# Hybrid decoder block: x in four half loads, row 0 ahead of the last transposes, and gated scores joined to the keys' transposes

## The chip, the cores and the metric

The kernel runs on one core of a Trainium2 chip. The metric is the device time of one execution in microseconds (us), lower is better. The kernel before was timed in three runs.

## What is computed

One decoder block over 256 tokens of width 1024, all in float32. Cut to what matters here:

```
h    = rms_norm(x, norm1_gain)              # x is 256 x 1024
proj = h @ w_in                             # 1024 x 3088, the first product
gq, gk, gv, gr, g_low, mq, mk, mv = split(proj)
log_a = log_sigmoid(g_low @ w_gate_up + b_gate) / 16
o_gla = gla_chunked(gq, gk, gv, log_a)      # gated linear attention, 4 heads: scores q_dec . k_inv, masked, times v
o_moba = attention(rotary(mq), rotary(mk), mv)   # 4 heads, causal over 256 tokens
x = x + concat(norm(o_gla) * silu(gr), norm(o_moba)) @ w_out
x = x + (silu(h2 @ w_gate) * (h2 @ w_up)) @ w_down    # h2 = rms_norm(x)
return rms_norm(x, final_norm_gain)
```

## The kernel before, in words

Every large product is done in three TensorE passes over fp32r parts: the left side is kept as a high and a low part (aT_hi, aT_lo), and so is each weight (w_hi, w_lo). A weight lands in a buffer `raw`, ScalarE casts it to w_hi, VectorE subtracts to get w_lo. Each product is therefore a triple hi*hi, hi*lo, lo*hi, of 512 columns each. Weights come in units of 2048 columns for each partition; raw has 3 slots and w_hi, w_lo have 6. A unit of w_in is 24 such matmuls for the two token tiles t = 0 and t = 1.

The order on each engine is written out by hand, and each engine waits on semaphores. There is no scheduler. The places that this study speaks of:

- The start. SyncE's queue issues x as two loads of 128 rows (`x_loaded`, L338), then the first eight rows of w_in one by one (`load_first`, L334): row 0 at once, rows 1 to 7 only when token tile 0 of x has landed. ("Row n" is one load of 128 x 512 weights.)
- TensorE first runs `warm_up` (L527), matmuls on constants whose result nobody reads, while x is on its way. Then it transposes x by 128 x 128 blocks into the aux banks (`x_transposed`, L535): block k of tile t goes to bank k // 2. Between the two tiles stand two small transposes, of norm1_gain (L543) and of the rotary frequencies (L546).
- ScalarE squares tile 0 (L885), then multiplies the transposed blocks by the gain into aT_hi (`take_xT`, L902), both token tiles of block k in one instruction, when the bank of both tiles is complete (`xT_in_psum`). VectorE makes w_hi and w_lo of row 0 (L1172, L1174) and aT_lo (L1157).
- `first_row(k)` (L564, L567, L570) multiplies block k of x by row k: two matmuls hi*hi, two hi*lo, two lo*hi. Behind row 0 stand `angle_inputs` (L553, L555), two small transposes.
- After row 7 come `gate_low` (L589), `other_gains` (L579), and then the units 2 to 11 of w_in (`in_unit`, L510 to L512). Between the matmuls of a unit's tile 0 and tile 1, or behind the unit, stand the attention steps, by the tables `midway` and `after`: `moba_k_transposed` (L613, eight 128 x 128 transposes of the rotated keys) midway in unit 7, and `gla_scores` (L650) behind it, `moba_scores` (L661, L665) midway in unit 8.
- gla_scores multiplies heads of 64 rows, so its weights are 64 partitions high. It waits for `glaT_ready`, which ScalarE signals after its copies L958. VectorE masks the result into a_gla (L1293, semaphore `a_ready`), and moba_scores waits for that, since it writes the same banks, and for `mT_q_ready` (ScalarE L975).

Of the kernel before, what the change touches and what calls it, by code (L numbers as in the profile page):

```python
# [22 lines left out]
P = 128  # L23
SEQ, D = 256, 1024
T = SEQ // P
# [67 lines left out]
def build_block(nc, x, positions, norm1_gain, w_in, w_gate_up, b_gate, gla_out_gain, moba_out_gain,  # L93
# [6 lines left out]
    with ExitStack() as ctx:  # L100
        def sb(name, shape, dt=f32):
            return ctx.enter_context(nc.sbuf_tensor(name, [P, *shape], dt))

        def sem(name):
            return ctx.enter_context(nc.semaphore(name))
# [8 lines left out]
        x_sb = sb("x_sb", [T, D])  # L114
# [93 lines left out]
        ang, turns, turns_lo, sin_arg = (reuse_e[:, n * T * HALF:(n + 1) * T * HALF] for n in range(4))  # L208


        x_loaded = [sem(f"x_loaded_{t}") for t in range(T)]
        rows_loaded = sem("rows_loaded")
        norm1_loaded = sem("norm1_loaded")
        low_loaded = sem("low_loaded")
# [117 lines left out]
        def _(sp):  # L332
            def load_first(n):
                sp.dma_start(raw[:, n // 4, (n % 4) * 512:(n % 4 + 1) * 512],  # L334
                             w_in[0, n * P:(n + 1) * P, BLOCKS[0]:BLOCKS[0] + 512]).then_inc(first_loaded[n], 16)

            for t in range(T):
                sp.dma_start(x_sb[:, t, :], x[0, t * P:(t + 1) * P, :]).then_inc(x_loaded[t], 16)  # L338
            load_first(0)
            sp.wait_ge(x_loaded[0], 16)  # L340
            for n in range(1, KC):
                load_first(n)

# [162 lines left out]
        def _(pe):  # L506
# [17 lines left out]
            def warm_up(n):  # L524

                for _ in range(n):
                    nc.tensor.matmul(acc[:, 2, 0:SEQ], warm[:, 0:P], warm, start=True, stop=True)  # L527

            warm_up(16)
            pe.wait_ge(ident_built, 1)  # L530

            def x_transposed(t, banks):
                for bank in banks:
                    for k in (2 * bank, 2 * bank + 1):
                        last = nc.tensor.transpose(aux[:, bank, (k % 2) * SEQ + t * P:(k % 2) * SEQ + (t + 1) * P],  # L535
                                                   x_sb[:, t, k * P:(k + 1) * P], ident[:, :])
                    if t == T - 1:
                        last.then_inc(xT_in_psum, 1)

            pe.wait_ge(x_loaded[0], 16)  # L540
            x_transposed(0, range(4))
            pe.wait_ge(norm1_loaded, 16)
            nc.tensor.transpose(acc[:, 3, NORM1_ROW:NORM1_ROW + KC], gain_rows[0:KC, :],  # L543
                                ident[0:KC, 0:KC]).then_inc(gains_in_psum, 1)
            pe.wait_ge(freq_loaded, 16)
            nc.tensor.transpose(acc[0:HALF, 0, 0:1], freq_row, ident[0:1, 0:1]).then_inc(freq_in_psum, 1)  # L546
            pe.wait_ge(x_loaded[1], 16)
            x_transposed(1, range(4))
            pe.wait_ge(gains_ready, 1)
            pe.wait_ge(freq_ready, 1)  # L550

            def angle_inputs():
                nc.tensor.transpose(freq, freq_col.to_broadcast([HALF, P]), ident[0:HALF, 0:HALF]).then_inc(freq_in_psum, 1)  # L553
                pe.wait_ge(pos_cast, 1)
                nc.tensor.transpose(acc[:, 3, KC:KC + T], pos_rows, ident[0:T, 0:T]).then_inc(pos_in_psum, 1)  # L555

            def first_row(k):

                right_hi, right_lo = weights(k // 4, 512, k % 4)
                toks = [slice(t * P, (t + 1) * P) for t in range(T)]  # L560
                pe.wait_ge(xT_hi_ready, k + 1)
                pe.wait_ge(first_hi_ready, k) if k else pe.wait_ge(row0_hi_ready, 1)
                for t in range(T):
                    nc.tensor.matmul(acc[:, t, :], aT_hi[:, k, toks[t]], right_hi, start=k == 0, stop=False)  # L564
                pe.wait_ge(first_lo_ready, k + 1)
                for t in range(T):
                    nc.tensor.matmul(acc[:, t, :], aT_hi[:, k, toks[t]], right_lo, start=False, stop=False)  # L567
                pe.wait_ge(xT_lo_ready, k + 1)
                for t in range(T):
                    last = nc.tensor.matmul(acc[:, t, :], aT_lo[:, k, toks[t]], right_hi, start=False, stop=k == KC - 1)  # L570
                    if k == KC - 1 and t == 0:
                        last.then_inc(tile0_in_psum, 1)
                if k % 4 == 3:
                    last.then_inc(unit_used, 1)
# [7 lines left out]
            def gate_low():  # L582


                pe.wait_ge(low_w_ready, 1)
                pe.wait_ge(xT_raw_ready, KC // 2)
                for k in range(KC):
                    group = slice(k % QUADS * SQUARE, (k % QUADS + 1) * SQUARE)
                    last = nc.tensor.matmul(aux[group, 2, 0:SEQ], low_w[:, k, :, :].rearrange("p w n -> p (w n)"),  # L589
                                            xT_raw[k // 2][:, k % 2 * SEQ:(k % 2 + 1) * SEQ], start=k < QUADS, stop=k >= QUADS)  # L590
                last.then_inc(low_in_psum, 1)
# [122 lines left out]
            def heads_transposed(group, banks):  # L714
                for t, bank in enumerate(banks):
                    n = 2 * group + t
                    pe.wait_ge(heads_ready, n + 1)
                    o = (o_moba, o_gla)[group]
                    transposes(bank, [o[:, t, h, :] for h in range(HEADS)]).then_inc(headsT_in_psum, 1)
# [62 lines left out]
            def ffn_phase(j, u, slot, parity, first=False):  # L782
# [2 lines left out]
                down((slot + 2) % RING, j, first=first)  # L785


            midway = {2: [logits], 7: [moba_k_transposed], 8: [moba_scores],
                      9: [probs_transposed], 10: [moba_outputs, gla_updates], 11: [gla_outputs, lambda: heads_transposed(0, (3, 0))]}
            after = {3: [cumulate], 7: [gla_scores]}  # L790
            for k in range(KC):
                first_row(k)
                if k == 0:
                    angle_inputs()
            gate_low()
            other_gains()
# [61 lines left out]
        def _(act):  # L858
# [25 lines left out]
            def sum_squares(norm, t):  # L884
                nc.scalar.activation(reuse_f[:, t * D:(t + 1) * D], x_sb[:, t, :], ACT.Square,  # L885
                                     accum_out=ss[:, norm, t:t + 1]).then_inc(ss_ready, 1)
# [21 lines left out]
                nc.scalar.copy(w_hi[:, n // 4, cols], raw[:, n // 4, cols]).then_inc(first_hi_ready, 1)  # L908


            act.wait_ge(x_loaded[0], 16)
            sum_squares(0, 0)
            act.wait_ge(gains_ready, 1)
            take_xT((0, 1))
# [628 lines left out]
```

## Time and profile before

| what | value |
|---|---|
| device time, median of 3 runs | 300.39 us (299.89 to 300.57) |
| device time of the profiled execution | 300.49 us |
| its span in the trace | 298.8 us |
| TensorE busy | 292.5 us, 98% of the span |
| VectorE busy | 240.4 us, 80% |
| ScalarE busy | 172.4 us, 58% |
| DMA | 55.49 MB moved, 186 GB/s on average |

The span is what the trace covers. The device time of the same execution is 1.7 us longer (300.49 less 298.8), for what lies before and behind it. Busy shares are averages over the whole program. The names of engines in the rows: PE is TensorE, PEld its weight loads, DVE VectorE, ACT ScalarE, SPq and ACTq the DMA queues of SyncE and ScalarE.

### The profile page before, as it was taken

What the parts mean: (1) busy time and instruction counts of PE and PEld (TensorE: products, weight loads), DVE (VectorE), ACT (ScalarE), POOL (GpSimd) and SP (SyncE); (2) the same over time, 40 slices, a digit from 0 to 9 for tenths busy, and PEclk for the clock granted to TensorE, in tenths of its full rate; (3) what the DMA queues carried; (4) which work ended last, traced back from release to release, by engine and by line L of the source; (5) the groups of instructions that cost most, each with busy time, mean ns of one, the idle gap of its engine ahead of it and who ended that gap; (6) DMA issues with size and microseconds to landing.
All of it is one profiled execution on the core that took longest, in us unless ns stands there. A gap on an engine that the chain in (4) does not pass through costs nothing.

```text
span 298.8 us, 4025 instructions
## 1 busy us (share of the span) xinstructions
PE 292.5 (98%) x1373; PEld 241.3 (81%) x1373; DVE 240.4 (80%) x401; ACT 172.4 (58%) x247; POOL 17.8 (6%) x40
## 2 busy tenths in 40 slices
PE   8999999999999999999999999999999999999992
PEld 6778888888898888887888888888888888888882
DVE  1999999777889687988888888979797978787155
ACT  3997799868765897717170808080808081713224
POOL 5120100000031001300000000000000000000002
PEclk9999999999999999999999999999999999999998
DMA  7997846737768122392929292919191919030003
GB/s 244 323 343 253 268 138 231 228 122 275 257 190 262 49 95 65 104 326 88 334 75 347 70 354 57 356 46 375 43 370 44 374 48 368 28 138 0 0 0 140
DMA packets 37382, 55.49 MB, mean 186 GB/s; under 512 B 2982, under 2 KB 26618, under 8 KB 37370
## 3 DMA queue, kind: packets, MB, share of 16 engines
q1 hardware_dynamic: 37204, 55.16, 54.9%
q8 instruction: 7, 0.11, 0.2%
q10 hardware_dynamic: 166, 0.17, 0.2%
q14 instruction: 5, 0.04, 0.0%
HBM read 53.75 MB, written 1.57 MB: 185 GB/s over the span
## 4 chain that ended last, share of the span: by engine, by line
PE 98%; DVE 0%; ACT 0%; issue 0%; DVEq 0%
PE acc L510 15%; PE acc L512 15%; PE acc L511 15%; PE aux L512 13%; PE aux L511 13%; PE aux L510 13%; PE aux L613 1%; PE acc L564 1%; PE acc L570 1%; PE acc L567 1%; PE acc L527 1%; PE aux L535 1%; PE aux L683 1%; PE aux L707 1%; PE aux L665 1%; PE aux L650 0%
## 5 line engine op out<-in xcount | busy, mean ns | idle before, releaser
L1153 DVE TENSOR_TENSOR w_lo<-raw,w_hi 128x2048 fp32r<-128x2048 f32 x46 | 103.4, 2286 | 16.0 <-ACT w_hi L879 15.9
L879 ACT CAST w_hi<-raw 128x2048 fp32r<-128x2048 f32 x46 | 85.9, 1908 | 4.7 <-DMA raw<-in_w_ffn_up 2.6
L510 PE MATMUL aux<-w_hi,aT_hi 128*128 128x512 f32 (+1 forms) x180 | 69.7, 387 | 0.0
L512 PE MATMUL aux<-w_hi,aT_lo 128*128 128x512 f32 (+1 forms) x180 | 69.6, 387 | 0.0
L511 PE MATMUL aux<-w_lo,aT_hi 128*128 128x512 f32 (+1 forms) x180 | 69.6, 387 | 0.0
L1455 DVE STREAM_TRANSPOSE reuse_c<-reuse_c 32x128 f32<-32x128 f32 x160 | 48.4, 303 | 2.4
L1091 ACT CAST pT_hi<-reuse_c 128x512 fp32r<-128x512 f32 x10 | 6.2, 621 | 72.8 <-DVE reuse_c L1455 72.8
L510 PE MATMUL acc<-w_hi,aT_hi 128*128 128x512 f32 x118 | 47.1, 399 | 0.0
L512 PE MATMUL acc<-w_hi,aT_lo 128*128 128x512 f32 x118 | 46.0, 390 | 0.0
L511 PE MATMUL acc<-w_lo,aT_hi 128*128 128x512 f32 x118 | 46.0, 390 | 0.0
L510 PEld LDWEIGHTS aux<-w_hi,aT_hi 128*128 128x128 f32 x180 | 33.8, 188 | 7.0
L511 PEld LDWEIGHTS aux<-w_lo,aT_hi 128*128 128x128 f32 x180 | 33.8, 188 | 6.9
L512 PEld LDWEIGHTS aux<-w_hi,aT_lo 128*128 128x128 f32 x180 | 33.8, 188 | 6.8
L510 PE MATMUL acc<-w_hi,pT_hi 128*128 128x512 f32 x80 | 31.3, 391 | 0.0
L512 PE MATMUL acc<-w_hi,pT_lo 128*128 128x512 f32 x80 | 31.2, 389 | 0.0
L511 PE MATMUL acc<-w_lo,pT_hi 128*128 128x512 f32 x80 | 31.1, 389 | 0.0
L512 PEld LDWEIGHTS acc<-w_hi,aT_lo 128*128 128x128 f32 x118 | 22.1, 188 | 4.8
L510 PEld LDWEIGHTS acc<-w_hi,aT_hi 128*128 128x128 f32 x118 | 22.2, 188 | 4.6 <-issue 0.2
L511 PEld LDWEIGHTS acc<-w_lo,aT_hi 128*128 128x128 f32 x118 | 22.2, 188 | 4.4
L1074 ACT ACTIVATE reuse_c<-aux,rstd 128x256 f32<-128x256 f32 x22 | 10.0, 472 | 19.2 <-PE aux L512 17.9
L510 PEld LDWEIGHTS acc<-w_hi,pT_hi 128*128 128x128 f32 x80 | 15.0, 188 | 3.4 <-issue 0.4
L512 PEld LDWEIGHTS acc<-w_hi,pT_lo 128*128 128x128 f32 x80 | 15.0, 188 | 3.1
(204 smaller groups left out, 282.2 us busy)
## 6 DMA issues: line engine op xcount, KB each, us to landing
raw<-in_w_ffn_gate SPq DMA_DIRECT2D x22, 512.0 KB, 4.1
raw<-in_w_ffn_up SPq DMA_DIRECT2D x22, 512.0 KB, 5.3
raw<-in_w_ffn_down SPq DMA_DIRECT2D x22, 512.0 KB, 5.9
raw<-in_w_in SPq DMA_DIRECT2D x20, 512.0 KB, 4.7
raw<-in_w_out SPq DMA_DIRECT2D x8, 512.0 KB, 4.4
raw<-in_w_in SPq DMA_DIRECT2D x8, 256.0 KB, 5.3
x_sb<-in_x SPq DMA_DIRECT2D x2, 512.0 KB, 3.9
m_moves<-reuse_c SPq DMA_DIRECT2D x1, 512.0 KB, 3.2
```

Source lines behind the costliest of these rows:

```text
L510: nc.tensor.matmul(dst, left_hi[:, k, tok], right_hi, start=first, stop=False)
L511: nc.tensor.matmul(dst, left_hi[:, k, tok], right_lo, start=False, stop=False)
L512: return nc.tensor.matmul(dst, left_lo[:, k, tok], right_hi, start=False, stop=last)
L527: nc.tensor.matmul(acc[:, 2, 0:SEQ], warm[:, 0:P], warm, start=True, stop=True)
L535: last = nc.tensor.transpose(aux[:, bank, (k % 2) * SEQ + t * P:(k % 2) * SEQ + (t + 1) * P], x_sb[:, t, k * P:(k + 1) * P], ident[:, :])
L564: nc.tensor.matmul(acc[:, t, :], aT_hi[:, k, toks[t]], right_hi, start=k == 0, stop=False)
L567: nc.tensor.matmul(acc[:, t, :], aT_hi[:, k, toks[t]], right_lo, start=False, stop=False)
L879: nc.scalar.copy(w_hi[:, slot % RING, :], raw[:, slot % RAW, :]).then_inc(hi_ready, 1)
L1074: nc.scalar.activation(silu_g[:, t, :], aux[:, GATE_UP_BANKS[parity][t], 0:FF], ACT.Silu, scale=rstd[:, 1, t:t + 1]).then_inc(silu_ready, 1)
L1091: nc.scalar.copy(dst, src.rearrange("p (k s) -> p k s", k=2)).then_inc(hiddenT_hi_ready, 1)
L1153: nc.vector.tensor_tensor(w_lo[:, slot % RING, :], raw[:, slot % RAW, :], w_hi[:, slot % RING, :].bitcast(f32), ALU.subtract).then_inc(lo_ ...
L1455: last = nc.vector.transpose(cols[SQUARE * c:SQUARE * (c + 1), :, :, g, :], rows[SQUARE * g:SQUARE * (g + 1), :, :, c, :])
```

## The change

x is loaded in four loads of 128 rows by 512 columns (left and right half of each tile), in the order tile 0 left, tile 0 right, tile 1 left, row 0 of w_in, tile 1 right. The waits for tile 0 become waits for both of its halves. TensorE runs 11 warm-up matmuls in place of 16. The transpose of norm1_gain moves ahead of x, the transposes of x are taken half by half, and those of tile 1's right half move behind row 0's products. gla_scores moves from behind unit 7 into its middle, right behind moba_k_transposed.

```
-        x_loaded = [sem(f"x_loaded_{t}") for t in range(T)]
+        x_loaded = [[sem(f"x{t}_{side}_loaded") for side in ("left", "right")] for t in range(T)]
...
-            for t in range(T):
-                sp.dma_start(x_sb[:, t, :], x[0, t * P:(t + 1) * P, :]).then_inc(x_loaded[t], 16)
+            def load_x(t, h):
+                sp.dma_start(x_sb[:, t, h * 512:h * 512 + 512], x[0, t * P:(t + 1) * P, h * 512:h * 512 + 512]).then_inc(x_loaded[t][h], 16)
+
+            load_x(0, 0)
+            load_x(0, 1)
+            load_x(1, 0)
             load_first(0)
-            sp.wait_ge(x_loaded[0], 16)
+            load_x(1, 1)
+            sp.wait_ge(x_loaded[0][0], 16)
+            sp.wait_ge(x_loaded[0][1], 16)
             for n in range(1, KC):
                 load_first(n)
...
-            warm_up(16)
+            warm_up(11)
             pe.wait_ge(ident_built, 1)
...
-            pe.wait_ge(x_loaded[0], 16)
-            x_transposed(0, range(4))
+            def x_half_transposed(t, h):
+                pe.wait_ge(x_loaded[t][h], 16)
+                x_transposed(t, (2 * h, 2 * h + 1))
+
             pe.wait_ge(norm1_loaded, 16)
             nc.tensor.transpose(acc[:, 3, NORM1_ROW:NORM1_ROW + KC], gain_rows[0:KC, :],
                                 ident[0:KC, 0:KC]).then_inc(gains_in_psum, 1)
+            x_half_transposed(0, 0)
+            x_half_transposed(0, 1)
             pe.wait_ge(freq_loaded, 16)
             nc.tensor.transpose(acc[0:HALF, 0, 0:1], freq_row, ident[0:1, 0:1]).then_inc(freq_in_psum, 1)
-            pe.wait_ge(x_loaded[1], 16)
-            x_transposed(1, range(4))
+            x_half_transposed(1, 0)
             pe.wait_ge(gains_ready, 1)
             pe.wait_ge(freq_ready, 1)
...
-            midway = {2: [logits], 7: [moba_k_transposed], 8: [moba_scores],
+            midway = {2: [logits], 7: [moba_k_transposed, gla_scores], 8: [moba_scores],
                       9: [probs_transposed], 10: [moba_outputs, gla_updates], 11: [gla_outputs, lambda: heads_transposed(0, (3, 0))]}
-            after = {3: [cumulate], 7: [gla_scores]}
+            after = {3: [cumulate]}
             for k in range(KC):
                 first_row(k)
                 if k == 0:
+                    x_half_transposed(1, 1)
                     angle_inputs()
...
-            act.wait_ge(x_loaded[0], 16)
+            for loaded in x_loaded[0]:
+                act.wait_ge(loaded, 16)
             sum_squares(0, 0)
```

TensorE's order at the start, before (aux is where x's transposes go, reuse_d holds norm1_gain, reuse_c the frequencies and positions):

```order
L527 MATMUL acc<-const-bfloat16-1.0 128x256 x16
L535 MATMUL aux<-ident,x_sb 128x128 x8
L543 MATMUL acc<-ident,reuse_d 128x8
L546 MATMUL acc<-ident,reuse_c 64x1
L535 MATMUL aux<-ident,x_sb 128x128 x8
L564 MATMUL acc<-w_hi,aT_hi 128x512 x2
L567 MATMUL acc<-w_lo,aT_hi 128x512 x2
L570 MATMUL acc<-w_hi,aT_lo 128x512 x2
L553 MATMUL acc<-ident,reuse_c 128x64
L555 MATMUL acc<-ident,reuse_c 128x2
```

The same stretch of the change, with the semaphores that each instruction waits for and its own line numbers (L533 is the warm-up, L541 the transposes of x, L573 to L579 row 0):

```order
1 L533 MATMUL acc<-const-bfloat16-1.0 128x256 x11
2 L551 MATMUL acc<-ident,reuse_d 128x8 [waits norm1_loaded,ident_built]
3 L541 MATMUL aux<-ident,x_sb 128x128 [waits x0_left_loaded]
5 L541 MATMUL aux<-ident,x_sb 128x128 [waits x0_right_loaded]
7 L556 MATMUL acc<-ident,reuse_c 64x1 [waits freq_loaded]
8 L541 MATMUL aux<-ident,x_sb 128x128 [waits x1_left_loaded]
10 L573 MATMUL acc<-w_hi,aT_hi 128x512 [waits xT_hi_ready,row0_hi_ready,freq_ready,gains_ready]
12 L576 MATMUL acc<-w_lo,aT_hi 128x512 [waits first_lo_ready]
14 L579 MATMUL acc<-w_hi,aT_lo 128x512 [waits xT_lo_ready]
16 L541 MATMUL aux<-ident,x_sb 128x128 [waits x1_right_loaded]
18 L562 MATMUL acc<-ident,reuse_c 128x64
```

Row 0's six matmuls now stand behind twelve transposes of x in place of sixteen, and the last four stand between row 0 and the angle inputs.

On SyncE's queue, before:

```order
1 L338 DMA x_sb<-in_x 128x1024 x2
2 L334 DMA raw<-in_w_in 128x512
3 L334 DMA raw<-in_w_in 128x512 [waits x_loaded_0]
```

and in the change:

```order
1 L338 DMA x_sb<-in_x 128x512 x3
2 L334 DMA raw<-in_w_in 128x512
3 L338 DMA x_sb<-in_x 128x512
4 L334 DMA raw<-in_w_in 128x512 [waits x0_right_loaded,x0_left_loaded]
```

Row 0 of w_in moves ahead of the last quarter of x; the wait ahead of row 1 is for the same data as before.

In unit 7, TensorE before (the rows between are the triples of tile 1, products 175 to 186):

```order
173 L512 MATMUL acc<-w_hi,aT_lo 128x512
174 L613 MATMUL aux<-ident,reuse_e 128x128 x8
175 L510 MATMUL acc<-w_hi,aT_hi 128x512
186 L512 MATMUL acc<-w_hi,aT_lo 128x512
187 L650 MATMUL aux<-glaT 128x128 x8
188 L510 MATMUL acc<-w_hi,aT_hi 128x512
```

and in the change (L622 are the keys' transposes, L659 the gated scores):

```order
174 L518 MATMUL acc<-w_hi,aT_lo 128x512
175 L622 MATMUL aux<-ident,reuse_e 128x128 x8
176 L659 MATMUL aux<-glaT 128x128 x8
177 L516 MATMUL acc<-w_hi,aT_hi 128x512
```

The gated scores moved ahead of the twelve products of tile 1 and stand directly behind the transposes. Nothing else changes its place on TensorE, and on VectorE, ScalarE and GpSimd nothing moves.

## Rows read from the trace of the kernel before

**Rows 1.** The page: engine totals, granted clock in 40 slices, and the chain's shares.
```profile
PE 292.5 (98%) x1373; PEld 241.3 (81%) x1373; DVE 240.4 (80%) x401; ACT 172.4 (58%) x247; POOL 17.8 (6%) x40
...
PEclk9999999999999999999999999999999999999998
...
PE 98%; DVE 0%; ACT 0%; issue 0%; DVEq 0%
```

**Rows 2.** Timeline of TensorE, 0 to 14 us: start, duration, engine, line.
```profile
0.83 3.57 PE L527 MATMUL acc<-const-bfloat16-1.0 128*128 128x256 bf16 x16 [0.83 <-PEq L1533]
4.40 1.94 PE L535 MATMUL aux<-ident,x_sb 128*128 128x128 f32 x8
6.27 0.27 PE L543 MATMUL acc<-ident,reuse_d 8*128 8x8 f32 x1
...
6.50 1.09 PE L535 MATMUL aux<-ident,x_sb 128*128 128x128 f32 x8
7.76 0.70 PE L564 MATMUL acc<-w_hi,aT_hi 128*128 128x512 f32 x2 [0.18 <-issue]
...
9.33 0.27 PE L553 MATMUL acc<-ident,reuse_c 64*128 64x64 f32 x1
...
9.68 0.73 PE L564 MATMUL acc<-w_hi,aT_hi 128*128 128x512 f32 x2
```

**Rows 3.** Timeline of TensorE in narrow windows: transposes of tile 0, second and seventh.
```profile
4.64 0.85 PE L535 MATMUL aux<-ident,x_sb 128*128 128x128 f32 x3
...
5.70 0.63 PE L535 MATMUL aux<-ident,x_sb 128*128 128x128 f32 x2
```

**Rows 4.** Timeline of ScalarE and VectorE, 0 to 20 us.
```profile
4.29 1.06 ACT L885 ACTIVATE reuse_f<-x_sb 128x1024 f32<-128x1024 f32 x1 [0.99 <-DMA x_sb<-in_x]
7.03 0.84 ACT L902 ACTIVATE aT_hi<-aux,gains 128x256 fp32r<-128x256 f32 x2 [1.60 <-PE aux L535]
...
6.99 0.41 DVE L1172 CAST w_hi<-raw 128x512 fp32r<-128x512 f32 x1
...
17.44 2.36 DVE L1209 TENSOR_TENSOR w_lo<-raw,w_hi 128x1024 fp32r<-128x1024 f32 x2
```

**Rows 5.** SyncE's queue: issue of the w_in rows, and row 0's time to landing.
```profile
1.71 5.76 SPq L334 DMA_DIRECT2D raw<-in_w_in  x8
...
raw<-in_w_in SPq DMA_DIRECT2D x1, 256.0 KB, 4.5
```

**Rows 6.** SyncE's queue from 0 to 2.95, 3.55, 4.20, 4.95 us: packets, MB.
```profile
q1 hardware_dynamic: 67, 0.27, 30.9%
...
q1 hardware_dynamic: 128, 0.50, 41.7%
...
q1 hardware_dynamic: 208, 0.79, 51.8%
...
q1 hardware_dynamic: 289, 1.05, 58.2%
```

**Rows 7.** The chain that ended last, 48 to 80 us: start, time, piece.
```profile
52.64 0.87 PE aux L613 x8
...
56.28 1.09 PE aux L650 x16
57.37 0.43 PE acc L510
...
60.32 0.89 PE aux L661 x8
...
77.88 0.59 PE aux L695 x8
```

**Rows 8.** Timeline of ScalarE and VectorE around units 7 and 8.
```profile
47.85 4.21 ACT L958 COPY glaT<-reuse_f 32x320 f32<-32x320 f32 x9
...
56.90 1.04 ACT L975 COPY reuse_f<-reuse_a 128x1024 f32<-128x1024 f32 x1
...
57.96 1.44 DVE L1293 COPY_PREDICATED reuse_b<-gla_mask,aux 128x256 f32<-128x256 int32 x4
```

## The prediction

> **What bounds the kernel now.** I read the page first. TensorE is busy for 98% of the span, and the chain that ended last runs through TensorE for 98% as well [rows 1]. So there is one rule for everything below: an edit gains only what it takes out of TensorE's own time line, either an idle stretch or a matmul that costs more than its columns. Work of the other engines counts only where TensorE would wait for it.
>
> The timeline of TensorE then shows where such time lies. At the start, 16 warm-ups fill 0.83 to 4.40 us, eight transposes of x follow at 4.40, two small ones from 6.27, eight more at 6.50, row 0 at 7.76, the angle inputs at 9.33, row 1 at 9.68 [rows 2]. From there TensorE runs without a gap. So the start of row 1, 9.68, is the mark: whatever row 1 starts earlier, with the same work behind it, is won, as long as no later wait takes it back.
>
> **The clock.** The granted clock stands at full on the page from the first slice [rows 1], yet the pace tells of two levels. Transposes two to seven of tile 0 start 0.212 us apart (4.64 to 5.70 for five steps) [rows 3]. Eight transposes of the same shape in unit 7 take 0.87 us, 0.109 each [rows 7]. The warm-ups, 256 columns each, take 0.223 [rows 2], which is 1.2 GHz. So TensorE is at the lower level (1.2 GHz) until at least 5.9 us and at the upper (2.4 GHz) by 6.5, when the second eight fit before 7.4. Before the rise it had been at work from 0.83 on with only a short gap near 4.3.
>
> **The start, step by step.** The first 0.27 MB on the queue have moved by 2.95 us and 0.50 MB by 3.55 [rows 6]; ScalarE starts on tile 0 (0.52 MB) at 4.29 [rows 4]. So a load can be used some 0.7 us after its last bytes moved. By the same lag tile 0's left half (0.26 MB) is there at 3.65, the right at 4.3, tile 1's left half (0.79 MB in all by 4.20) at 4.9, and row 0 of w_in (1.05 MB by 4.95) at 5.65. Row 0 lands at 1.71 + 4.5 = 6.2 now [rows 5].
>
> TensorE with the change. Eleven warm-ups end at 0.83 + 11 x 0.223 = 3.3 and cost nothing, since x isn't there yet. The gain's transpose falls into the idle time behind them. Tile 0's eight transposes start at 3.75 (0.1 behind the landing, as now) and take 8 x 0.213 = 1.7 at the lower level, to 5.45; the right half, there at 4.3, is in time for 4.6. The two small transposes and their switches take 0.39 now (4.40 + 8 x 0.213 = 6.11, to 6.50); one of them is gone, and I take 0.3. Tile 1's left half starts at 5.75, 0.85 behind its landing. ScalarE started 0.53 behind the first of these transposes (6.50 to 7.03) [rows 2, 4] when two of them took 0.22; at the lower level two take 0.43, so ScalarE starts at 5.75 + 0.74 = 6.49. Row 0's products came 0.73 behind ScalarE's start (7.03 to 7.76), so they come at 7.22 in place of 7.76: 0.54 us earlier. VectorE's cast of row 0 came at 6.99 and ended at 7.40, 0.36 ahead of the products; now it can start about 6.1, so it isn't in the way.
>
> Row 0 lasts 1.57 (7.76 to 9.33) and the angle inputs 0.35 [rows 2]. Between them now stand four transposes: 0.44 at the upper level by the unit 7 price [rows 7], with 0.05 for the switch. Row 0 has less to wait for, since both halves of its weights are ready earlier; six matmuls at 0.227 would be 1.36, and I take 1.45. Row 1 starts at 7.22 + 1.45 + 0.49 + 0.35 = 9.51, which is 0.17 earlier; with a rise of the clock during tile 1's left half, or a half that lands a tenth earlier, it is up to 0.4. I take **0.25 us**.
>
> Bounds of this term. Below: the halves land no earlier than the whole (twice as many packets, each half as long), row 0 stays at 7.76, and the four moved transposes cost 0.49: a loss of 0.5. Above: the clock is up early enough that only data counts, and row 0's weights (5.65, plus 0.41 for the cast and 0.36) allow 6.4: a gain of 7.76 - 6.4 - 0.49 = 0.9.
>
> Does what follows keep up? Rows 1 to 7 are issued when tile 0 is there, the same moment as now. VectorE's low part of unit 2 ends at 17.44 + 2.36 = 19.8 and is bound by its load; TensorE needs it at 20.6. That margin of 0.8 is the narrowest I find up to unit 4, and 0.25 fits in.
>
> **The join in unit 7.** The chain gives the keys' transposes 0.87 for eight, next to no overhead, and the gated scores 1.09 for sixteen, then 0.43 for the first product behind them, where a product costs 0.23 [rows 7]. The scores' own columns take about what eight transposes take, 0.85, as two 64-row matmuls go side by side; so they carry 0.24 on entry and 0.20 on exit. The exit stays, since a product still follows. For the entry the nearest row is L695 in unit 10, which changes shape right behind another fp32 group: 0.59 for four matmuls' 0.43, or 0.16 on entry. So the join saves 0.24 - 0.16 = 0.08, and perhaps a few hundredths that the products lose behind the transposes. I take **0.1 us**, with bounds 0 and 0.28 (the whole entry).
>
> The Trainium skill, "TensorEngine Tiling (Array Packing)", Key Properties, says that a change of the tiling mode drains TensorE. The trace agrees in that only L650 and the product behind it carry the extra 0.24 and 0.20. By the rule alone the join would save nothing, since the change of mode stands on both sides of the scores either way, and the sum would be 0.25 in place of 0.35.
>
> Who is late next: the scores need glaT, ready at 47.85 + 4.21 = 52.06 [rows 8]. TensorE reaches them at 52.64 + 0.87 - 0.25 = 53.26, so they wait for nothing. The end of unit 7 comes about 1.0 us later, and with it the second half of ScalarE's take of mv, which ends at 56.90 now; the copy L975 behind it ends at 57.94 now and about 58.6 then. VectorE's masks end at 57.96 + 1.44 = 59.40 [rows 8]. moba_scores starts at 60.32 [rows 7] and wants both; 0.35 earlier it is 59.97, still 0.5 behind the masks. The join thus costs nothing there.
>
> **The sum.** 0.25 + 0.1 = 0.35 us off 300.49 for the profiled execution, 300.14. The median is 300.39, 0.1 below that execution, so I forecast 300.0. A difference of under 0.2%, 0.6 us, can't be told from no change here.
>
> **The rivals.**
>
> *The clock rises later* (chance 0.12). Now TensorE has an idle stretch from 3.3 to 3.75, where it had warm-ups, and a second one of 0.6 ahead of row 0. If the level stays at 1.2 GHz past row 0's start, each microsecond there yields half its work. The gain of 0.35 is gone after 0.7 us, and 0.6 us slower needs 1.9 us, to about 9.1. If it holds to the end of row 1 near 10, the loss is 1.3 and the time 301.3. For it: five warm-ups fewer before the rise. Against it: transposes take their place half a microsecond later, and near 4.3 there was a gap too. The Trainium skill, "TensorE: Matmul & The Clock Gate", What's actually happening, says that the array's clock follows how busy TensorE has lately been and that the point of the rise moves from run to run. The trace shows one rise only, so it neither bears this out nor denies it.
>
> *The halves don't land earlier* (0.12). Twice as many packets for the same bytes, or the frequencies' load, which TensorE now wants at 5.45 and not at 6.4, holds up the chain. Then row 0 stays near 7.76 and the moved transposes cost 0.49; with the join's 0.1 that is 300.8, and 300.4 if half of it holds. It ends as no change.
>
> *Better than forecast* (0.16). The clock is up by 5.5, or the first half lands near 3.3. Then ScalarE starts before 6.0 and row 0 at 6.5 to 6.7; row 1 gains 0.6 to 0.8, and with the join it is 299.5.
>
> *The change as summed* (0.60): 300.0, its own range 299.6 to 300.4.
>
> **How the numbers follow.** Over 0.6 us faster, below 299.8: all of the third rival and a quarter of the forecast's own range, 0.31. Slower than 301.0: most of the first rival and a little of the second, 0.12. The rest, 0.57, is within 0.2%. The range goes from 299.3, the third rival and its join, to 300.9, the second's worst case, and leaves out the late clock.
>
> **What would show it.** Right: the first transposes near 3.75, row 0 near 7.2 behind some 0.6 us of idle time, row 1 at 9.3 to 9.6, first product behind the joined group still with 0.2 extra, and moba_scores starting with no gap. Wrong: transposes of the last quarter 0.21 apart (the clock), a first transpose at 4.2 or later (the loads), an idle gap ahead of L541 of tile 1's left half (frequencies or load), or ahead of unit 2 or moba_scores (margins used up).

## The result and the profile after

The change is slower: 301.34 us median (300.03 to 303.13, 22 executions) against 300.23 (299.70 to 300.64, 22 executions). The ratio is 1.0039, with a 95% interval of 1.0025 to 1.0053. I had forecast 300.0, in 299.3 to 300.9, and gave slower by over 0.2% a chance of 0.12. The spread says as much as the median: 3.1 us in place of 0.9. The profiled execution, 303.13 us with a span of 301.4, is the longest of the 22. And even the shortest, 300.03, lies behind the shortest of before, 299.70.

TensorE's timeline of the change from the start, as [rows 2] (start, duration, engine, line of its own kernel: L533 warm-ups, L551 the gain, L541 x's transposes, L573 to L579 the products, L562 the angle inputs):

```profile
0.83 2.50 PE L533 MATMUL acc<-const-bfloat16-1.0 128*128 128x256 bf16 x11 [0.83 <-PEq L1544]
3.27 0.27 PE L551 MATMUL acc<-ident,reuse_d 8*128 8x8 f32 x1
3.47 2.17 PE L541 MATMUL aux<-ident,x_sb 128*128 128x128 f32 x8
...
6.07 1.12 PE L541 MATMUL aux<-ident,x_sb 128*128 128x128 f32 x4 [0.29 <-DMA x_sb<-in_x]
7.59 1.19 PE L573 MATMUL acc<-w_hi,aT_hi 128*128 128x512 f32 x2 [0.40 <-ACT aT_hi L912]
8.58 1.05 PE L576 MATMUL acc<-w_lo,aT_hi 128*128 128x512 f32 x2
9.43 1.05 PE L579 MATMUL acc<-w_hi,aT_lo 128*128 128x512 f32 x2
10.29 1.05 PE L541 MATMUL aux<-ident,x_sb 128*128 128x128 f32 x4
11.27 0.37 PE L562 MATMUL acc<-ident,reuse_c 64*128 64x64 f32 x1
...
11.76 1.22 PE L573 MATMUL acc<-w_hi,aT_hi 128*128 128x512 f32 x2
...
13.77 0.62 PE L573 MATMUL acc<-w_hi,aT_hi 128*128 128x512 f32 x2
```

Row 1 starts at 11.76 in place of 9.68 [rows 2], 2.08 us later, and row 1 itself lasts 2.01 us (to 13.77) where it lasted 1.49 (to 11.17 in the trace of before). These two, 2.60, are all but 0.04 of the 2.64 us between the two profiled executions (303.13 less 300.49).

Read the pace of the pairs. L576 starts at 8.58 and L579 at 9.43, so two matmuls of 512 columns take 0.85 us, 0.43 each: the 1.2 GHz level. From 13.77 on such a pair takes 0.46. So TensorE was at the lower level through x's transposes, row 0, the four moved transposes (0.98 us with their switch, where I had 0.49) and most of row 1, until some time after 12.8. In before it was at 2.4 GHz by 6.5.

ScalarE's and VectorE's timeline, where [rows 4] stood for before:

```profile
4.57 1.06 ACT L895 ACTIVATE reuse_f<-x_sb 128x1024 f32<-128x1024 f32 x1 [1.28 <-DMA x_sb<-in_x]
...
6.86 0.84 ACT L912 ACTIVATE aT_hi<-aux,gains 128x256 fp32r<-128x256 f32 x2 [1.14 <-PE aux L541]
...
6.69 0.43 DVE L1183 CAST w_hi<-raw 128x512 fp32r<-128x512 f32 x1 [0.51 <-DMA raw<-in_w_in]
```

The loads, where [rows 5] and [rows 6] stood: the time to landing of tile 1's left half, issued at 1.71, and what the queue had moved by 4.95 us:

```profile
x_sb<-in_x SPq DMA_DIRECT2D x1, 256.0 KB, 4.3
...
q1 hardware_dynamic: 480, 0.89, 58.0%
```

By 4.95 us only 0.89 MB had moved, not 1.05 [rows 6]. Between 3.55 and 4.95 the core's DMA ran at 271 GB/s, where before it ran at 394. Tile 1's left half was usable at 6.03 us; in before the whole of tile 1 was there at 5.55. Row 0's weights came at 6.69; before they were there at 6.2 [rows 5].

These two delays follow from when the loads are issued. SyncE's queue before, and the time to landing of the whole tile 1, issued at 1.24:

```profile
0.80 0.86 SPq L338 DMA_DIRECT2D x_sb<-in_x  x2
...
x_sb<-in_x SPq DMA_DIRECT2D x1, 512.0 KB, 4.3
```

The same queue in the change, and the time to landing of row 0's weights, issued at 2.17:

```profile
0.80 1.33 SPq L338 DMA_DIRECT2D x_sb<-in_x  x3
2.17 0.43 SPq L334 DMA_DIRECT2D raw<-in_w_in  x1
...
raw<-in_w_in SPq DMA_DIRECT2D x1, 256.0 KB, 4.5
```

Each issue keeps the queue busy for 0.38 to 0.43 us, whether it is for a whole tile or for half of one, and the next comes 0.44 to 0.48 behind it. Tile 1's left half is the third load (1.71), where the whole tile 1 was the second (1.24). Both took 4.3 us to land. Row 0's weights are the fourth (2.17), where they were the third (1.71), and took 4.5 both times.

The chain through units 7 and 8, as [rows 7] (L622 the keys' transposes, L659 the gated scores, L670 the next scores):

```profile
55.26 0.87 PE aux L622 x8
56.13 1.09 PE aux L659 x16
57.22 0.43 PE acc L516
...
62.93 0.89 PE aux L670 x8
```

The joined scores cost the same 1.09, and the product behind them the same 0.43. From the transposes to the next scores it is 7.67 us (55.26 to 62.93), against 7.68 (52.64 to 60.32) [rows 7]. The join moved 0.01 us.

### The profile page after: what moved, and what is told of

It is laid out like the page before. It is cut to its first block, busy times and chain, and to the rows that moved or that the text cites. A ratio compares the mean times of both kernels' runs of the same rounds, so it can differ in the third digit from the quotient of the medians.

```text
span 301.4 us, 4019 instructions
## 1 busy us (share of the span) xinstructions
PE 294.6 (98%) x1368; PEld 242.7 (81%) x1368; DVE 240.8 (80%) x401; ACT 172.6 (57%) x247; POOL 17.4 (6%) x40
## 4 chain that ended last, share of the span: by engine, by line
PE 96%; DMA 1%; ACT 1%; DVE 0%; issue 0%; SPq 0%; DVEq 0%; ACTq 0%
PE acc L516 15%; PE acc L518 15%; PE acc L517 15%; PE aux L518 13%; PE aux L516 13%; PE aux L517 13%; PE acc L573 2%; PE aux L622 1%; DMA x_sb<-in_x 1%; PE acc L576 1%; PE acc L579 1%; PE aux L692 1%; PE aux L716 1%; PE aux L674 1%; PE aux L541 1%; PE aux L659 0%
```

## The experiments

Each was run with the kernel before on the same chip, and the ratio is to that. For a quick reading I use one mark: when row 1 starts on TensorE. In every profiled execution where the clock was up by then, row 1's start plus 290.8 us gives the device time within 0.1 us (before: 9.68 and 300.49). Everything behind row 1 is the same.

| kernel | median us (executions) | ratio to before, 95% | row 1 in the profile | that execution |
|---|---|---|---|---|
| the change, 11 warm-ups | 301.34 (22) | 1.0039 (1.0025 to 1.0053) | 11.76 | 303.13 |
| the change again | 301.89 (12) | 1.0057 (1.0030 to 1.0083) | 11.01 | 301.81 |
| before_warm11 | 301.39 (6) | 1.0035 (1.0021 to 1.0049) | 10.71 | 301.54 |
| after_warm16 | 300.71 (11) | 1.0017 (1.0008 to 1.0026) | 9.87 | 300.71 |
| gaps_filled | 300.71 (12) | 1.0029 (1.0016 to 1.0042) | 9.84 | 300.61 |
| join_only | 300.08 (11) | 0.9996 (0.9986 to 1.0005) | 9.62 | 300.46 |
| halves_only | 300.70 (11) | 1.0026 (1.0017 to 1.0035) | 10.52 | 301.38 |
| rows64 | 302.95 (6) | 1.0091 (1.0072 to 1.0110) | 12.06 | 302.90 |
| order_only | 300.10 (12) | 1.0010 (1.0000 to 1.0019) | 9.25 | 300.06 |
| moved_only | 300.76 (11) | 1.0019 (1.0002 to 1.0035) | 10.02 | 300.82 |
| gain_first | 300.16 (11) | 1.0003 (0.9994 to 1.0012) | 9.54 | 300.43 |
| before_warm20 | 300.56 (12) | 1.0019 (1.0010 to 1.0029) | 9.21 | 300.04 |
| left_right | 303.72 (6) | 1.0123 (1.0107 to 1.0138) | 10.18 | 301.00 |

None is faster than the kernel before beyond its interval. The ratio weighs all executions, so it need not be the quotient of the two medians.

**Five warm-ups fewer, alone.**

```
-            warm_up(16)
+            warm_up(11)
```

> The kernel before with 11 warm-up matmuls in place of 16, nothing else. Theory A (the clock: five warm-ups fewer delay TensorE's rise to 2.4 GHz): 300.7 to 302.5 us, with runs that spread over 1 to 3 us instead of the 0.9 us of the kernel before. Theory B (the half loads and the new order cost the time, by tile 1's left half landing at 6.03 us): the same as before within 0.1%, 300.2 us, and the same spread.

TensorE's timeline of the first 12 us of this kernel:

```profile
4.24 1.94 PE L535 MATMUL aux<-ident,x_sb 128*128 128x128 f32 x8 [0.90 <-DMA x_sb<-in_x]
...
6.36 1.97 PE L535 MATMUL aux<-ident,x_sb 128*128 128x128 f32 x8
7.98 1.20 PE L564 MATMUL acc<-w_hi,aT_hi 128*128 128x512 f32 x2
...
10.71 0.72 PE L564 MATMUL acc<-w_hi,aT_hi 128*128 128x512 f32 x2
```

Theory A held in the time. TensorE's timeline shows tile 1's transposes at the lower level (1.97 us for eight, where before took 1.09) and most of row 0 too. Whole loads, before's order, and yet row 1 comes 1.03 later than in the profile of before. Five matmuls on constants, whose result nobody reads, are worth 0.35% here, 1.05 us by the ratio (the medians are 301.39 and 300.17). The spread of its six executions, 1.09 us, is no wider than that of before on the same chip, 0.99, so the spread that theory A asked for isn't shown by this run.

**The change with 16 warm-ups.**

```
-            warm_up(11)
+            warm_up(16)
```

> The change with 16 warm-up matmuls put back, nothing else. Theory A (the clock): 300.0 to 300.4 us and a spread under 1 us. Theory B (the loads and the order): 301 us or more, since the half loads are still there and five more warm-ups even start the first transposes at 4.4.

TensorE's timeline of this kernel, same stretch:

```profile
4.25 1.09 PE L541 MATMUL aux<-ident,x_sb 128*128 128x128 f32 x8
...
5.97 0.66 PE L541 MATMUL aux<-ident,x_sb 128*128 128x128 f32 x4 [0.52 <-DMA x_sb<-in_x]
7.32 0.70 PE L573 MATMUL acc<-w_hi,aT_hi 128*128 128x512 f32 x2 [0.69 <-DVE w_hi L1183]
...
8.99 0.60 PE L541 MATMUL aux<-ident,x_sb 128*128 128x128 f32 x4
...
9.87 0.73 PE L573 MATMUL acc<-w_hi,aT_hi 128*128 128x512 f32 x2
```

The median fell to 300.71 and the spread to 0.6 us (300.24 to 300.88). So the five warm-ups, by way of the clock, are over half of the loss (0.22 of 0.39%), but 0.17% stays. Both theories had part of it: A's spread, and neither A's 300.0 to 300.4 nor B's 301. Here the clock is up from the first transpose (eight in 1.09), and still row 0 waits 0.52 for tile 1's left half and 0.69 for VectorE's cast of row 0's weights, which waited for their load. Row 1 is at 9.87, later than in before, whose clock rose two microseconds later.

**The same number of warm-ups, placed in the gaps.**

```
             nc.tensor.transpose(acc[0:HALF, 0, 0:1], freq_row, ident[0:1, 0:1]).then_inc(freq_in_psum, 1)
+            warm_up(2)
             x_half_transposed(1, 0)
+            warm_up(3)
             pe.wait_ge(gains_ready, 1)
```

> The change with 11 warm-ups at the start, and two more warm-up matmuls ahead of tile 1's left half and three ahead of row 0, so as many as before, but in the idle stretches. Theory A in the form 'the idle stretches between 5.4 and 7.6 us keep the clock down': about 300.2 with a spread under 1 us. In the form 'the work up to 4.4 us decides': still 301 or more with a spread over 2 us. Theory B (loads): 301 or more, a narrow spread.

Nine of twelve executions lie at 300.5 to 300.9, three at 301.5 to 302.5. Neither form of theory A describes that. Nor is it shown that work in the gaps helps: the interval, 1.0016 to 1.0042, overlaps the change's own, 1.0025 to 1.0053. In the profile the two added matmuls of 256 columns at 5.81 already take 0.29 us together, the upper level, so in that execution the clock had risen before the first of them. What stands is that the same five matmuls ahead of x give the narrower spread, 0.6 us in place of 2.1.

**The join, alone.**

```
-            midway = {2: [logits], 7: [moba_k_transposed], 8: [moba_scores],
+            midway = {2: [logits], 7: [moba_k_transposed, gla_scores], 8: [moba_scores],
...
-            after = {3: [cumulate], 7: [gla_scores]}
+            after = {3: [cumulate]}
```

> The kernel before with only the gated scores joined to the keys' transposes. My prediction gave this 0.1 us (300.1); the profile of the change says 0.01 (7.67 us in place of 7.68 from the transposes to the next scores), so 300.2. Theory C, that the join delays work and costs something: 300.4 or more, with an idle gap of TensorE in units 7 to 9.

No difference that can be told: 0.9996, though an interval of 0.9986 to 1.0005 doesn't exclude the 0.1 us that I had forecast. The chain does: here too it is 7.67 us from the transposes to the next scores. The join neither gains nor costs more than 0.01 us there.

**Half loads, alone.** x in four half loads, 16 warm-ups, before's order. The waits for a tile ask for 32 in place of 16, both of its halves.

```
             for t in range(T):
-                sp.dma_start(x_sb[:, t, :], x[0, t * P:(t + 1) * P, :]).then_inc(x_loaded[t], 16)
+                for h in range(2):
+                    sp.dma_start(x_sb[:, t, h * 512:h * 512 + 512], x[0, t * P:(t + 1) * P, h * 512:h * 512 + 512]).then_inc(x_loaded[t], 16)
```

> The kernel before, 16 warm-ups and its own order, with x in four half loads (tile 0 left, right, tile 1 left, right, then row 0) and the waits for both halves. Theory D (the half loads, 2 KB a row in place of 4 KB, move slower: in the change 0.89 MB by 4.95 us in place of 1.05): tile 0 lands 0.2 to 0.5 us later, tile 1 at 6.1 to 6.6 in place of 5.55, row 1 starts 0.3 to 0.7 later than 9.68, and the time is 300.5 to 300.9. Theory E (what was left of the loss with 16 warm-ups lies in TensorE's order or in row 0 being moved ahead): 300.2, as before.

TensorE's timeline of this kernel, and behind it the DMA queue's row up to 4.95 us (packets, MB, share of the engines' time):

```profile
7.21 1.09 PE L536 MATMUL aux<-ident,x_sb 128*128 128x128 f32 x8 [1.30 <-DMA x_sb<-in_x]
8.48 0.70 PE L565 MATMUL acc<-w_hi,aT_hi 128*128 128x512 f32 x2 [0.18 <-DVE w_hi L1173]
...
10.52 0.74 PE L565 MATMUL acc<-w_hi,aT_hi 128*128 128x512 f32 x2
```

The queue:

```profile
q1 hardware_dynamic: 472, 0.87, 53.7%
```

Theory D held in the time: the half loads alone cost 0.26%. TensorE stood idle for 1.30 us until tile 1 was there at 7.2, not 6.1 to 6.6, and the queue had moved 0.87 MB by 4.95 (second fence). But this profile is of the second longest of 11 executions, 301.38; by the mark the median has row 1 near 9.9 and not at 10.52. Tile 0 was not late at all: ScalarE starts on it at 4.28, in before at 4.29. Tile 1's last half is the fourth issue, at 2.19, 0.95 behind the whole tile 1 of before, and took 5.0 us to land in place of 4.3. So 0.95 us of its delay is the later issue and 0.7 a longer landing.

**Four loads of full rows.** Is it the short rows?

```
+                for h in range(2):
+                    sp.dma_start(x_sb[h * 64:h * 64 + 64, t, :], x[0, t * P + h * 64:t * P + h * 64 + 64, :]).then_inc(x_loaded[t], 16)
```

> The kernel before with x in four loads as well, but each of 64 rows in full width, 4 KB a row, 256 KB as the half loads. If the short rows make them slow (theory D1): landing as before, 300.2 us, and 1.05 MB moved by 4.95. If it is the number of loads and issues (theory D2): as slow as the half loads, 300.5 to 300.9.

The same two views of this kernel:

```profile
5.73 1.06 PE L536 MATMUL aux<-ident,x_sb 128*128 128x128 f32 x8 [1.39 <-DMA x_sb<-in_x]
...
7.81 1.97 PE L536 MATMUL aux<-ident,x_sb 128*128 128x128 f32 x8 [0.84 <-DMA x_sb<-in_x]
9.43 1.20 PE L565 MATMUL acc<-w_hi,aT_hi 128*128 128x512 f32 x2
```

The queue:

```profile
q1 hardware_dynamic: 194, 0.66, 59.0%
```

D1 fell: with 4 KB a row the four loads are slower still, 0.66 MB by 4.95 (second fence), and the loss is 0.91%, beyond D2's figure too. The first fence shows TensorE's level fall back as well: tile 0's eight transposes take 1.06, tile 1's take 1.97, with 1.39 and 0.84 us of idle time ahead of them. So part of this loss is the clock's again. Here the page records it: the granted clock, which reads 9 in the second slice (7.5 to 15 us) of every other profile, reads 7.

```profile
PEclk9799999999999999999999999999999999999999
```

Over 8.00 to 10.00 us it is 0.50, over 6.00 to 7.50 and over 11.00 to 13.00 it is 1.00. These loads were also the slowest to issue, 0.56 to 0.60 us each; the fourth came at 2.67 and took 5.1 to land.

**The change's order with whole loads and 16 warm-ups.**

```
-            load_x(0, 0)
-            load_x(0, 1)
-            load_x(1, 0)
+            for t in range(T):
+                sp.dma_start(x_sb[:, t, :], x[0, t * P:(t + 1) * P, :]).then_inc(x_loaded[t][0], 16)
             load_first(0)
-            load_x(1, 1)
...
-            warm_up(11)
+            warm_up(16)
```

> The change's order on TensorE with 16 warm-ups, but x in its two whole loads, row 0 of w_in behind them. Theory D (loads): row 0 of w_in lands at 6.1 as before, row 0's products start near 7.1 and row 1 at 9.2 to 9.5, so 299.8 to 300.0 us, 0.2 to 0.4 faster than before. Theory E (the order costs): 300.4 to 300.8.

TensorE's timeline of this kernel:

```profile
4.43 1.09 PE L538 MATMUL aux<-ident,x_sb 128*128 128x128 f32 x8
...
6.85 0.70 PE L570 MATMUL acc<-w_hi,aT_hi 128*128 128x512 f32 x2 [0.61 <-ACT aT_hi L909]
...
8.37 0.60 PE L538 MATMUL aux<-ident,x_sb 128*128 128x128 f32 x4
...
9.25 0.74 PE L570 MATMUL acc<-w_hi,aT_hi 128*128 128x512 f32 x2
```

These lines are against the change, so the joined scores and the early gain are in it. The profile is what theory D asked for, row 0 at 6.85 and row 1 at 9.25. The time isn't: 300.10, where before had 299.83 on that chip, though the interval of the ratio just reaches 1.0000. The clock was up at 4.4 in this execution, while in the profile of before it rose near 6.2. Before's own shortest executions, 299.6 to 299.8, would then have row 1 near 8.9 by the mark (299.7 less 290.8), an estimate, since no profile here caught one. From row 0's start to row 1's it is 2.40 us here, 1.92 in before. So even with whole loads and a sure clock this order doesn't win, and the next run says why.

**Only the four transposes behind row 0.**

```
-            x_transposed(1, range(4))
+            x_transposed(1, range(2))
...
                 if k == 0:
+                    x_transposed(1, range(2, 4))
                     angle_inputs()
```

> The kernel before, whole loads and 16 warm-ups, with only tile 1's right four blocks transposed behind row 0's products in place of ahead of them. Theory E' (these 0.44 us were hidden in the idle time ahead of row 0, and behind it nothing hides them): 0.1 to 0.4 us slower than before, most so in the executions with an early rise, so the fastest ones are at 300.0 and not at 299.7. Theory F (they were on the path before, so moving them costs nothing and row 0 comes earlier by as much): as before or up to 0.2 faster.

TensorE's timeline of this kernel:

```profile
6.37 0.66 PE L535 MATMUL aux<-ident,x_sb 128*128 128x128 f32 x4
7.68 0.70 PE L564 MATMUL acc<-w_hi,aT_hi 128*128 128x512 f32 x2 [0.65 <-ACT aT_hi L903]
...
9.15 0.60 PE L535 MATMUL aux<-ident,x_sb 128*128 128x128 f32 x4
...
10.02 0.73 PE L564 MATMUL acc<-w_hi,aT_hi 128*128 128x512 f32 x2
```

Theory E' held in its sign: 0.19% slower (0.57 us, where it had 0.1 to 0.4), shortest execution 300.26 where before's was 299.73. Row 0 starts at 7.68, as in before (7.76), since ScalarE needs only the first bank, which was always transposed first. What was 0.18 us idle ahead of row 0 is 0.65 now, and row 1 is 0.34 later. One execution of the eleven took 302.85; its mean granted clock, 0.990, is the lowest of them (the others have 0.995 or more). A fall of the level like that in rows64 would do this, but no profile shows it.

**Only the gain's transpose ahead of x.**

```
+            pe.wait_ge(norm1_loaded, 16)
+            nc.tensor.transpose(acc[:, 3, NORM1_ROW:NORM1_ROW + KC], gain_rows[0:KC, :],
+                                ident[0:KC, 0:KC]).then_inc(gains_in_psum, 1)
             pe.wait_ge(x_loaded[0], 16)
             x_transposed(0, range(4))
```

> The kernel before with only norm1_gain's transpose moved ahead of x. It takes about 0.2 us from between tile 0 and tile 1 into the wait for x. With a late rise row 0 starts about 0.2 earlier, with an early one row 0's weights bind it anyway: 0 to 0.15 us faster than before in the median. If it costs (by another switch of weights ahead of x): 0.1 slower.

No difference that can be told, 1.0003 (0.9994 to 1.0012). A gain of up to 0.15 us, as I had expected, would not show in it.

**More warm-ups, 20 in place of 16.**

```
-            warm_up(16)
+            warm_up(20)
```

> The kernel before with 20 warm-ups, which end near 5.1 us. If more work ahead makes the clock's rise earlier or surer: 299.9 to 300.2 us with a spread under 0.7 us, since the transposes start later but run at 2.4 GHz. If 16 were enough already: 300.2 to 300.6, since tile 0 waits for the warm-ups.

TensorE's timeline of this kernel:

```profile
4.89 1.03 PE L535 MATMUL aux<-ident,x_sb 128*128 128x128 f32 x8
...
7.31 0.70 PE L564 MATMUL acc<-w_hi,aT_hi 128*128 128x512 f32 x2 [0.18 <-issue]
```

The profiled execution is early (row 1 at 9.21), but the kernel is 0.19% slower than before by the ratio, inside the second of the two expectations. In the executions in which the clock is not up by 4.3, the four more are at the lower level too and tile 0 waits for them: my reading of the spread, 299.93 to 300.92, not shown by a profile.

**Two loads, by halves of both tiles.** Left halves, row 0's weights, right halves; eight transposes on each side of row 0. The joined scores and the gain ahead of x are in it too, and ScalarE's squares of tile 0 come behind its first two blocks.

```
+                sp.dma_start(x_sb[:, :, h * 512:h * 512 + 512],
+                             x[0, :, h * 512:h * 512 + 512].rearrange("(t p) n -> p t n", p=P)).then_inc(x_loaded[h], 16)
```

> x in two loads, the left half of both tiles, then row 0 of w_in, then the right half; rows of 2 KB but only two loads of 512 KB. TensorE: 16 warm-ups, the eight left transposes, row 0, the eight right ones; ScalarE squares tile 0 behind its first two blocks. If short rows make the half loads slow (D1), the left load lands at 4.5 to 4.7 us and the right near 6.6, and row 1 starts at 9.5 or later: 300.1 or more. If the number of loads does (D2), they land at 4.3 and by 6.2, row 0 starts near 6.4, row 1 near 9.1, and the time is 299.7 to 300.0. Theory E', that work moved behind row 0 costs its full 0.11 us a transpose once the clock is up early, adds 0.4 to either, as the idle time ahead of row 0 no longer covers it.

TensorE's timeline of this kernel:

```profile
5.11 1.09 PE L539 MATMUL aux<-ident,x_sb 128*128 128x128 f32 x8 [0.55 <-DMA x_sb<-in_x]
...
7.19 0.70 PE L571 MATMUL acc<-w_hi,aT_hi 128*128 128x512 f32 x2 [0.87 <-DVE w_hi L1181]
```

The left load was usable at 5.1, later than either theory said, although only two loads of x were issued. It was issued at 0.80 like the first load of before and has the same 512 KB, and took 4.3 us to land in place of 3.5. So neither the issue nor D2 is the cause by itself either. The profiled execution was the best of six, 301.00; four of the others lie at 303.7 to 304.1.

**The change once more.**

> The change itself once more, for a second profile beside the first and for its spread on this chip. Theory A: a median of 300.8 to 302 us and a spread of 1.5 to 3 us, and in the profile the device time follows the moment of the rise: row 1's start plus 290.8 (300.49 less 9.68) gives the time within 0.1 to 1.2 us, the rest being products of rows 1 to 7 still at 1.2 GHz.

TensorE's timeline of this second profile of the change:

```profile
3.49 1.97 PE L541 MATMUL aux<-ident,x_sb 128*128 128x128 f32 x8
...
7.69 1.19 PE L573 MATMUL acc<-w_hi,aT_hi 128*128 128x512 f32 x2 [0.40 <-ACT aT_hi L912]
...
10.14 0.60 PE L541 MATMUL aux<-ident,x_sb 128*128 128x128 f32 x4
...
11.01 0.73 PE L573 MATMUL acc<-w_hi,aT_hi 128*128 128x512 f32 x2
```

Same kernel, another moment of the rise. Here the moved transposes already run at the upper level (0.53 to the next instruction), so the rise came near 9.9, not past 12.8, and the time is 301.81, which is 11.01 + 290.8. The median, 301.89, is as expected. The twelve executions spread from 300.08 to 303.63, 3.55 us, a little more than the 3 that I had allowed.

## Why the prediction was wrong

**What bounds the kernel** was right: TensorE's own line, with row 1's start as the mark. It gave each profiled time within 0.1 us where the clock was up by then; in the change's own profile row 1 itself was slow too, and the time is 0.57 above the mark.

**The step that cost most: the warm-ups at nothing.** I wrote that eleven warm-ups "cost nothing, since x isn't there yet", and called the transposes half a microsecond later a replacement for the other five. before_warm11 shows that they are not: it has no new order and no half loads, and loses 0.35%. From row 0's start to row 1's I had 2.29 us (1.45 + 0.49 + 0.35); the profile has 4.17 (7.59 to 11.76), and row 1 another 0.5 on top. Of the 2.25 us by which row 1 missed my 9.51, 1.88 are this. I had the rival's place, its price and its sign, with 301.3 for the whole, and gave it 0.12; that the median came out at 301.34 is luck, since the moment of the rise differs from execution to execution and the loads and the order have a part in that median. With 16 warm-ups at the start the executions of before, after_warm16, join_only, halves_only, order_only and gain_first spread over 0.6 to 1.1 us; those of the change and of gaps_filled, with 11, over 2.1 to 3.6. There are exceptions both ways: before_warm11 has 1.1, moved_only with 16 has 2.6 by one execution, and rows64 and left_right with 16 have 1.5 and 3.1, where loads left TensorE idle. The Trainium skill, "TensorE: Matmul & The Clock Gate", What's actually happening, says that the point of the rise moves from run to run, and gives half a microsecond either way. The two profiles of the change agree that it moves, but by about 3 us: near 9.9 in one, past 12.8 in the other. Here the measurement decides.

**The step that failed first in time: the issue of a load, put at nothing.** I took the bytes that the queue had moved with two whole loads [rows 6], added the 0.7 us lag, and read off tile 1's left half at 4.9 and row 0's weights at 5.65. That supposes that four loads move bytes as two do, and it leaves out that each is issued in its turn, 0.44 to 0.48 us behind the one ahead. They were there at 6.03 and 6.69, 0.5 later than in before: one more turn each, with the same 4.3 and 4.5 us from issue to landing. The rows had it: row 0's 4.5 from its issue [rows 5], carried over to the issue at 2.17, gives 6.7. I had priced late halves as a lower bound (row 0 at 7.76), with a chance of 0.12 and no row for it. halves_only shows half loads alone, at 0.26%. The steps between were right: ScalarE 0.79 behind the first of the transposes (I had 0.74), row 0's products 0.73 behind ScalarE (0.73). Row 0 came at 7.59 in place of my 7.22, and 0.29 of these 0.37 us is TensorE's wait for the left half. It was still 0.17 earlier than in before.

**The moved transposes.** Their 0.49 was right at the upper level (0.53 in after_warm16, 8.99 to 9.52). But I set them against a gain that needed early data. Without it they lose: moved_only, 0.19%. In before they stood in the shadow of ScalarE's 0.73 us; I had seen the idle time ahead of row 0 grow to 0.6 and took no lesson from it.

**The join** was sized 0.1 and is 0.01. The step that failed is the entry's 0.16 taken from L695; the entry behind the transposes costs the 0.24 that it cost behind the products. The Trainium skill, "TensorEngine Tiling (Array Packing)", Key Properties, says that a change of the tiling mode drains TensorE. The trace agrees: the scores still cost 1.09 and the product behind them 0.43, since the join leaves a change of mode on both sides of them.

**Adding up.** The change's order costs 0.10% (order_only), half loads on top bring it to 0.17% (after_warm16), and five warm-ups fewer to 0.39%. The first two intervals overlap (1.0000 to 1.0019 and 1.0008 to 1.0026), so what the half loads add inside the change isn't shown by these medians. The last step is nearly clear of the one ahead of it (1.0025 to 1.0053) and clear in the change's second set (1.0030 to 1.0083).

**What stays open.** Why a load sometimes takes longer from issue to landing. In the change, its second profile, after_warm16 and gaps_filled tile 1's left half takes 4.2 to 4.4 and row 0's weights 4.5 to 4.6, as in before, so the later issue is all of it. In halves_only row 0's weights took 5.2, in rows64 5.1, and in left_right the first load took 4.3 in place of 3.5; the issue doesn't explain these. Nor do the bytes moved: between 3.55 and 4.95 us they are about 390 and 350 GB/s with two loads of x (before; left_right, 0.34 to 0.83 MB), 271 and 217 with four (the change; rows64, 0.36 to 0.66 MB), but gaps_filled, with the change's own loads, ran at 181 and landed them as the change did. left_right also began later, with 0.14 MB by 2.95 against 0.27, and I have one profile of most. The Trainium skill, "DMA: Bandwidth & Descriptors", Measured, advises transfers of 1 MiB and more because small ones lose efficiency. It measured single transfers issued from GpSimd, not several in flight from SyncE, and no run here isolates that mechanism.

Open too is which property of the five warm-ups the clock answers to. before_warm11 takes them away and leaves TensorE idle for 0.90 us ahead of x; in the change transposes follow at once (3.47), and the level is late all the same. No run tells whether transposes do less for the clock than those matmuls, or whether it is the idle time of 0.29 and 0.40 us further on.

## What to carry to other kernels

Warm-up matmuls at a kernel's start are not idle filling: before you take some out because the data comes sooner, time the kernel with only that edit, and look at many executions, not at one profile. Don't read the landing of a split load off the byte curve of the whole one: count from its own turn to be issued, and profile the split by itself. And before moving work from ahead of a wait to behind it, ask whether the wait covered it: idle time that grows by as much as you moved away is the sign that nothing was won.

## What the runs showed of the hardware

- The profile doesn't show the first rise of the clock. In before and in the change the granted clock is 1.00 in every window at the start, while matmuls of 512 columns take 0.43 us in one stretch of the change and 0.23 in another. There the level has to be read from the pace. The fall and second rise in rows64 are recorded (0.50 over 8.00 to 10.00 us).
- With the level once up it fell back within the start: in rows64 eight transposes take 1.06 us at 5.73 and 1.97 at 7.81, with 0.84 us of idle time directly ahead and 1.39 ahead of the first.
- SyncE's queue issued a load of x or of row 0 every 0.44 to 0.48 us in before and in the change, and one of 512 KB took it no longer than one of 256 KB (0.42 us each, the second loads of before and of the change). In rows64, with 64 rows to a load, it was every 0.61 to 0.64.
- Four loads of 256 KB brought the first quarter early (used from 3.5 us in the change) and everything behind it late: the second at 4.4, where the whole tile 0 was there at 4.3 in before, the third at 6.0.
